# Two joined pairs of chunks in each feed-forward, and the joining copies on ScalarE

## The reference

```python
def swiglu_ffn(h, w_gate, w_up, w_down):
    return (jax.nn.silu(h @ w_gate) * (h @ w_up)) @ w_down

for l in range(DEPTH):                       # first block; the second one ends its layers in the same way
    h = rms_norm(x, norm_pre[l, 0])
    x = x + 0.5 * rms_norm(swiglu_ffn(h, ffn1_w_gate[l], ffn1_w_up[l], ffn1_w_down[l]), norm_post[l, 0])
    ...                                      # mixer, second feed-forward
```

## Time and profile before

| | us |
|---|---|
| median of 3 runs | 2022.09 (2021.98 to 2022.65) |
| the profiled execution's own time | 2023.4 |
| its span | 2021.6 |
| TensorE busy | 2000.0 |
| VectorE busy | 1589.3 |
| ScalarE busy | 1169.2 |

### The profile page before, as it was taken

How to read it: one execution, slowest core, us unless ns; L and a number is a source line. 1 busy time by engine, 2 the same in 40 slices (tenths; PEclk the granted TensorE clock), 3 DMA queues, 4 the chain that set the end, 5 groups by cost and what they waited for, 6 DMA issues and landing times.

```text
span 2021.6 us, 24239 instructions
## 1 busy us (share of the span) xinstructions
PE 2000.0 (99%) x9442; PEld 1639.1 (81%) x9442; DVE 1589.3 (79%) x2024; ACT 1169.2 (58%) x1438; POOL 0.2 (0%) x4
## 2 busy tenths in 40 slices
PE   8999999999999999999999999999999999999998
PEld 6788887888888888887888888888888887888887
DVE  6896899778867877899768967966788679667885
ACT  6455657664546555666564646756645466566453
POOL 0000000000000000000000000000000000000000
PEclk9999999999999999999999999999999999999999
DMA  8766764567777675764557767554667674546764
GB/s 261 235 204 183 225 201 146 171 194 208 221 211 240 202 229 171 225 189 146 186 184 208 223 184 212 189 157 148 191 214 215 190 226 161 176 141 186 223 211 121
DMA packets 339122, 394.54 MB, mean 195 GB/s; under 512 B 123824, under 2 KB 235072, under 8 KB 339008
## 3 DMA queue, kind: packets, MB, share of 16 engines
q1 hardware_dynamic: 334912, 381.94, 61.8%
q10 hardware_dynamic: 4096, 11.05, 1.5%
HBM read 365.66 MB, written 1.05 MB: 181 GB/s over the span
## 4 chain that ended last, share of the span: by engine, by line
PE 88%; DVE 6%; DMA 2%; ACT 2%; issue 1%; SPq 1%; ACTq 0%; DVEq 0%
PE ps L739 75%; PE ps L876 5%; DVE w_lo L2113 2%; PE ps L810 1%; DVE scratch L2530 1%; DMA raw<-in_ffn_w_up 1%; PE ps L1361 1%; PE ps L1342 1%; DVE x L2163 0%; ACT w_hi L1421 0%; DMA raw<-in_w_co 0%; DVE scratch L2567 0%; PE ps L925 0%; PE ps L833 0%; DMA x<-in_x 0%
## 5 line engine op out<-in xcount | busy, mean ns | idle before, releaser
L2113 DVE TENSOR_TENSOR w_lo<-raw,w_hi 128x2048 fp32r<-128x2048 f32 x336 | 766.3, 2286 | 135.2 <-ACT w_hi L1421 133.2
L1421 ACT ACTIVATE w_hi<-raw 128x2048 fp32r<-128x2048 f32 (+2 forms) x340 | 643.6, 1897 | 378.5 <-PE ps L739 169.9
L739 PE MATMUL ps<-w_hi,hT_hi 128*128 128x512 f32 x1856 | 731.5, 394 | 0.0
L739 PE MATMUL ps<-w_lo,hT_hi 128*128 128x512 f32 x1856 | 723.5, 390 | 0.0
L739 PE MATMUL ps<-w_hi,hT_lo 128*128 128x512 f32 x1856 | 699.4, 389 | 0.0
L739 PEld LDWEIGHTS ps<-w_hi,hT_hi 128*128 128x128 f32 x1856 | 348.9, 188 | 75.8 <-issue 5.5
L739 PEld LDWEIGHTS ps<-w_hi,hT_lo 128*128 128x128 f32 x1856 | 348.4, 188 | 73.4
L739 PEld LDWEIGHTS ps<-w_lo,hT_hi 128*128 128x128 f32 x1856 | 349.1, 188 | 69.6
L739 PE MATMUL ps<-w_hi,bT_hi 128*128 128x512 f32 x608 | 239.8, 394 | 0.6 <-DVE bT_lo L2204 0.5
L739 PE MATMUL ps<-w_hi,bT_lo 128*128 128x512 f32 x608 | 236.9, 390 | 0.0
L739 PE MATMUL ps<-w_lo,bT_hi 128*128 128x512 f32 x608 | 236.8, 390 | 0.0
(11 more groups left out here) (340 smaller groups left out, 1742.4 us busy)
## 6 DMA issues: line engine op xcount, KB each, us to landing
raw<-in_w_in SPq DMA_DIRECT2D x160, 512.0 KB, 4.6
raw<-in_ffn_w_down SPq DMA_DIRECT2D x88, 512.0 KB, 4.4
raw<-in_ffn_w_gate SPq DMA_DIRECT2D x86, 512.0 KB, 4.1
raw<-in_ffn_w_up SPq DMA_DIRECT2D x86, 512.0 KB, 5.0
raw<-in_w_gate SPq DMA_DIRECT2D x44, 512.0 KB, 4.0
raw<-in_w_up SPq DMA_DIRECT2D x44, 512.0 KB, 5.0
raw<-in_w_down SPq DMA_DIRECT2D x44, 512.0 KB, 4.5
raw<-in_w_out SPq DMA_DIRECT2D x32, 512.0 KB, 4.2
```

Of the source, the lines that this page charges most:

```text
L739: mm = nc.tensor.matmul(bank(t, half), act[:, tiles[i], t * P:(t + 1) * P], w, start=start and (i, n) == steps[0], stop=stop and (i, n) == ...
L1421: nc.scalar.activation(dst, src, ACT.Copy).then_inc(high_ready, 1)
L2113: V.tensor_tensor(lo, src, flat(hi), ALU.subtract).then_inc(low_ready, 1)
```

## The change

`PAIRS` names the first chunks of the joined pairs: chunks 3 and 4 are one now, chunks 6 and 7 another, with chunk 5 plain between them. `JOIN_ON_ACT` takes the two copies of each `join` from VectorE to ScalarE (`join_here`). `HOOK` and one condition in ScalarE's part move work on tables for the second block by one chunk. Since the first pair starts at chunk 3, its row sums move ahead: `rows_whole` and `row_sums` around the product of chunk 1, `sum_hi` ahead of chunk 2. On SP, the transposes of a second half now stand behind the load of the next block 1.

```diff
--- before.py
+++ after.py
@@ -58,9 +58,9 @@
 NEG = -1e30
 
 
-PAIRS = (5,)
-JOIN_ON_ACT = False
-HOOK = 7
+PAIRS = (3, 6)
+JOIN_ON_ACT = True
+HOOK = 8
 
 
 def _ffn_order():
@@ -596,10 +596,8 @@
             def pair(c):
                 if c - 3 in PAIRS:
                     turn_halves(L, n, c - 3)
-                    turn_halves(L, n, c - 2)
                 square(L, k0 + AT["p", c, 1], wg, 0, c * FC)
-                if c - 3 not in PAIRS:
-                    turn_halves(L, n, c - 2)
+                turn_halves(L, n, c - 2)
                 square(L, k0 + AT["p", c, 7], wu, 0, c * FC)
                 square(L, k0 + AT["p", c, 3], wu, 512, c * FC)
                 square(L, k0 + AT["p", c, 2], wg, 512, c * FC)
@@ -1619,6 +1617,9 @@
                 hidden(0)
             silu(L, k0 + 3, 1)
             high(L, k0 + 4 + AHEAD)
+            if PAIRS[0] == 3:
+                act.wait_ge(*after("forms", "rows", f))
+                nc.scalar.activation(sum_hi[:, :, :], sums, ACT.Copy).then_inc(*done("held", "rows_high", f))
             for c in range(2, NCHUNK - 1):
                 if c in SECOND:
                     continue
@@ -1633,7 +1634,7 @@
                     at, width = CONST["inv_freq"]
                     for at, end in ((P, at), (at + width, CONST_ARRAY.shape[1])):
                         act.dma_start(const[:, at:end], d["const"][:, at:end]).then_inc(const_loaded, 16)
-                if L.sub0 + j == 0 and c == 8:
+                if L.sub0 + j == 0 and c == 9:
                     rope()
                 if memory_here(L, n) and c == (9 if NCHUNK - 3 in SECOND or NCHUNK - 4 in SECOND else 8):
                     memory_std(L.l)
@@ -2374,8 +2375,12 @@
                 join(0)
                 hidden_low(0)
             weight_low(L, k0 + 3 + AHEAD)
+            if PAIRS[0] == 3:
+                rows_whole()
             hidden(1)
             part(1)
+            if PAIRS[0] == 3:
+                row_sums()
             weight_low(L, k0 + 4 + AHEAD)
             for c in range(2, NCHUNK - 1):
                 if c in SECOND:
```

## The result

The changed kernel takes 2070.69 us (median of 4 runs, 2068.95 to 2073.09) against 2022.05: ratio 1.0241, 95% interval 1.0223 to 1.0258. It is 48.6 us slower. The direction was forecast; the time (2036, 2014 to 2048) was not.

A forecast was written before the change was run, and what follows sets the result against it. TensorE, busy 99%, was taken as the bound. Pair waits less the saving and removed waits gave +1.94 us in five feed-forwards and +4.14 in one, together +13.8, so 2036 us, range 2014 to 2048.

The forecast's parts named there:

- The saving: TensorE's work in the second pair: seven blocks replace eight, gaining 2.51 us in each of six feed-forwards, 15.1 us.
- 15 us from `t1` to block 2, so `t1` is wanted 9.6 us ahead of block 1: VectorE's fixed order from the first weight combination to block 2's low part takes 15.1 us, 5.5 of them after block 1.
- First pair, late by 2.6 (4.8 in two): Chunks 3 and 4: block 2 waits 2.6 us by ScalarE's chain, 4.8 in two feed-forwards where VectorE starts 2.2 later.
- The upper bound of 3.6: Highest lateness allowed for first pairs (5.8 in two feed-forwards) in the sum's upper bound of +26 us, 2048.
- Second pair, "late by 2.2 to 3.3 us, and take 2.2": Chunks 6 and 7: `t1` waits for block 7's weights and comes 2.2 to 3.3 us late; 2.2 us taken.
- The issue at X + 9.4: Block 7's load goes out on SP's queue, behind the transposes, 9.4 us after X, the start of plain chunk 5.
- the lower bound of 5 us: Block 7's load, from issue to `t1`, bounded by 5 and 6.15 us; 5 gives `t1` at 14.4 us after chunk 5's start.
- VectorE's own bound, X + 12.0: Second pair: VectorE alone could begin `t1` 12.0 us after chunk 5's start X, late by nothing against 12.2 wanted.
- Joins elsewhere "at nothing": Joining copies moved to ScalarE outside the pairs cost nothing, since TensorE does not wait for VectorE there.
- The estimate of 0.61 us: One ScalarE copy of 512 elements per the skill's formula; a 0.63 us row agreed, and 1.1 us was taken for two.
- Everything else is paid for by waits: Beyond the 15.1 us saving, every other effect was priced as TensorE waits, since TensorE has no other slack.

The follow-up runs named there:

- first_only: The changed kernel without its second pair, so only chunks 3 and 4 are joined; 26 us slower than the kernel before.
- mended: Changed kernel: second pair's first steps earlier, high-part matmuls first, chunk 0's joins on VectorE, first pair's `t1` ahead of hidden low part; 16 us above its expected 2014 to 2026.

## Why the prediction was wrong in size

- *The saving.* Right: 15.1 forecast, 16.3 by the count of starts.
- *15 us from `t1` to block 2, so `t1` is wanted 9.6 us ahead of block 1.* Right in both pairs (15.1 and 15.2).
- *First pair, late by 2.6 (4.8 in two).* Right in sum, 20.0 against 20.8, partly by luck. ScalarE's chain set `t1` as forecast (VectorE is idle 1.15 us for it at 1509.39). Of the 3.1 us here 0.9 stand at block 1: chunk 2's product on VectorE was in my list, but not as something that block 1 waits for. The two feed-forwards with 4.8 (the first one and that at 1028 us) have 3.3 each; in the first one 2.1 us stand earlier, at the opening. The third has 4.7 and 0.4 more, from a load of memory rows that I had not placed. The upper bound of 3.6 has no working.
- *Second pair, "late by 2.2 to 3.3 us, and take 2.2".* Mis-sized: the second pairs waited 24.1 us against 13.2. The issue at X + 9.4 was exact, and `t1` did wait for the load. Two readings failed. First, I took the lower bound of 5 us for the load where the trace had 6.15, because the next load seemed to go out back to back there. That was a misreading of the merged row: it went out 5.4 us later there, and 1.9 us later here. From issue to `t1` block 7's load took 5.1 to 6.15 us in the six pairs before and 6.0 to 8.0 in the second pairs; the DMA share here was 0.56 before (1495.2 to 1501.4) and 1.12 after. Second, VectorE's own bound, X + 12.0, let the second hidden low part wait for nothing. It waits for the transposes, the joins and ScalarE's high part (idle 2.65 us at 1560.37) and ends at X + 15.1: even a load of 5 us would have brought `t1` forward by 0.3 us only.
- *Joins elsewhere "at nothing".* Right with one pair. Here the openings' waits were left out: 2.9 us behind the joins of chunk 0, and 2.7 where `rows_whole` stands ahead of chunk 1's product (2.1 of them in the first feed-forward). So were 1.8 us at the first feed-forward's down unit, beside the small loads. Two copies took 1.39 us, not 1.1, and 0.77 each on average. The estimate of 0.61 us by the Trainium skill, "ScalarE: Activation LUTs", section "What ACT_TABLE_LOAD costs", was low too.
- *The step that failed most: the sum priced waits alone.* "Everything else is paid for by waits" had no term for TensorE's clock behind them, 17.2 us of half-clock distances; filling the waits took 14.3 of them away and gave 12 us back. The row that misled me is the wait of 2.2 us in the earlier trace rows, behind which the clock stayed up.

10.9 (second pairs), 17.2 (clock) and 7.3 (openings, down unit) make 35.4 us, and the forecast missed by 34.7. That they agree so well is in part chance: smaller terms of either sign, 1 to 4 us each (the table's rest, waits outside the feed-forwards, the openings' waits of before, the larger saving), nearly cancel.

## What to carry to other kernels

Where TensorE is the bound and a change makes it wait, price the wait and then the matmuls behind it at half the clock; one wait that did no such harm is no proof. When a load decides a start, take its time from the trace at a place as crowded as the new one, and list every transfer that other engines issue in that stretch. A late step in a chain of engines moves its wait to the next unit when one place is mended, so run the mends together before judging a layout: this one went from 49 us slower to even, and what was left in its first pairs was VectorE's.

## What the hardware showed that was not expected

- The clock does not follow one wait alone. In the kernel before a wait of 2.2 us left it at 1.00. In the changed kernel five first pairs had waits of 0.8 to 1.1 and 2.2 us, 7.6 us apart. Behind four of them it stood at 0.66 over the next 5 us, behind the fifth (1932.58) at 1.00. In `first_only` nearly the same two waits brought it down in one of five feed-forwards, and in `mended` single waits of 2.2 to 2.8 us at the down unit in one of four. What decides was not settled.
- A 16-bit copy of 128x512 in a permuted order took 0.77 us on ScalarE and 0.45 on VectorE; a 32-bit copy of as many elements took 0.63 on ScalarE.
